# Sixteen ring slots: a 4 KB transfer scratch for GpSimd, and the norms' weight rows in the projection's output

## The chip, the cores and the metric

One core of one Trainium2 chip runs the kernel. The metric is device time in microseconds (us); the time before is the median of three runs. The engines named below are TensorE (PE, with its weight loads as PEld), VectorE (DVE), ScalarE (ACT), GpSimd (POOL) and SyncE (SP). SyncE issues nearly all transfers, GpSimd some fifty small ones.

## The reference

Everything is float32, with 256 tokens of width 1024. The first block is a hybrid layer with a mixture of experts, the second has two layers with a dense feed-forward each. Cut to what matters:

```python
# first block
mod = silu(c) @ w_ada + b_ada                      # six vectors of 1024
proj = (rms_norm(x, norm1_g) * (1 + scale1) + shift1) @ w_in
y = concat(conv(proj), stick_breaking(proj), forgetting(proj))
x = x + gate1 * ((head_rms(y) * out_norm_g) @ w_out)
h2 = rms_norm(x, norm2_g) * (1 + scale2) + shift2
for e in range(32):                                # top 4 of 32 for each token
    u = h2 @ w_mlp1[e] + b_mlp1[e]                 # 1024 x 2048
    acc += gate[e] * (swiglu(u) @ w_mlp2[e] + b_mlp2[e])   # 1024 x 1024
x = x + gate2 * acc
# second block
x = x + concat(fnet(p), conformer_conv(p)) @ w_out_ab     # p = rmsnorm(x) @ w_in_ab
x = x + swiglu_ffn(rmsnorm(x), w_gate, w_up, w_down)      # 1024 x 2816
x = x + pool_mixer(rmsnorm(x), pool_map) * pool_scale
x = x + swiglu_ffn(rmsnorm(x), w_gate, w_up, w_down)
return rmsnorm(x, final_g)
```

## The kernel before

All weights pass through one ring in SBUF. It has NRING slots of UNIT = 2048 float32 a partition, which is 1 MiB each. `ring_order` writes down, ahead of time, the order of all units and for each unit its slot, the semaphore value at which it has landed, and the units that held its slot before. A unit that is `wide` (all expert weights but the last expert's w2) takes two neighbouring slots and is one transfer of 2 MiB. SyncE goes through the same order: `fill` (line 3111 issues) waits until the slot's former units are emptied, and starts the transfer. It issues in order, so a fill that waits holds up all behind it. PE, DVE and ACT wait for a unit by its slot's semaphore.

The program runs through these parts:

- The front uses slots 0 to 7 for w_ada, w_in, then scale2, w_out. Slots 8 to 13 hold scratch of the front until its projection is done: `hTH`, `hTL` and the pieces `wp` of w_in, split in two rounded parts. `sp.wait_ge(*done(("in", "used", 31)))` stands ahead of gate2, which goes to slots 8 to 11.
- The experts: e = 0 to 31, in the order w1 of e (rows 2, 4, 6), the first w1 of e + 1, then the two w2 of e. Six wide units belong to one expert. TensorE (line 936 for w1, 954 for w2) multiplies up to 64 tokens of an expert, and up to 32 more in a second pass where it has them.
- The second block: w_in_ab (`abc`, `abr`), dft, fnet_map, w_out_ab, and gate, up and down of each feed-forward. It rotates through seven slots, since slots 7 to 13 hold the split hidden activations `FTH`, `FTL` and `HTH`.

Beside the ring lies one arena, a tensor of AW float32 a partition from which `al` hands out pieces. `o_rows` is the piece for seven norm weight vectors, one a partition. GpSimd loads them first (`small("rows", ...)`, line 2991), and TensorE turns them into columns at lines 585 and 588, before the modulation's last part and the projection. `o_P` is the piece `PJ`, the projection's output of 6144 float32 a partition. The rest of the arena is in use from front to end in changing roles.

GpSimd's own transfers are written by software into a descriptor scratch at the start of SBUF, 16 KB a partition by default. Its loads are the rows, biases and small vectors at the start, then the cumulated gates, the router's weights, and from 153 us the expert biases in_b_mlp (b1 and b2). ScalarE waits for b1 at line 2631, between its splits of the output projection's pieces.

```python
units[name] = (s, 16 * uses[s], [b for b in dict.fromkeys(before) if b is not None])
...
for prior in before:
    for step in emptied(prior):
        sp.wait_ge(*done(step))
sp.dma_start(view(ring[:, s * UNIT:(s + 1 + wide(name)) * UNIT]), src).then_inc(s_slot[s], 16)
```

Of the kernel before, what the change touches and what calls it, by code (L numbers as in the profile page):

```python
# [11 lines left out]
ACT = mybir.ActivationFunctionType  # L12
AX = mybir.AxisListType.X

NRING = 14
UNIT = 2048
NEXP = 32
CAP = 64
# [95 lines left out]
def w2_order(e):  # L114

    return (0, 2, 1, 3) if e == NEXP - 1 else (0, 2)


def wide(name):

    return name[0] == "w1" or name[0] == "w2" and name[1] < NEXP - 1


def front_order():

    order = []
    for n in range(16):
        order.append(("in", n // 2, n % 2))
        if 2 <= n < 10:
            order.append(("ada", 1, n - 2))  # L130
    return order


def ring_order():

    order = [("ada", 0, k) for k in range(8)] + front_order()
    first = len(order)
    order += [("scale2", k) for k in range(4)] + [("out", kk) for kk in range(4)] + [("gate2", k) for k in range(4)]
    experts = len(order)
    order += [("w1", 0, 0)]  # L140
    for e in range(NEXP):
        order += [("w1", e, k) for k in (2, 4, 6)]
        if e + 1 < NEXP:
            order += [("w1", e + 1, 0)]
        order += [("w2", e, k) for k in w2_order(e)]
    post = len(order)
    order += [("abc", c) for c in AB] + [("abr", kk) for kk in range(2)] + [("dft",), ("fm",)]
    order += [("outab", kk) for kk in range(4)]
    for l in range(2):
        if l:  # L150
            order += [("pool",), ("pmap",)]
        order += [(w, l, j) for j in range(NFF // 2) for w in ("gate", "up")]
        order += [("down", l, kk) for kk in range(NFF // 2)]
    units, uses, prior, at = {}, [0] * NRING, [None] * NRING, 0
    slots = list(range(8))
    for n, name in enumerate(order):
        if n == first:
            assert at % 2 == 0
            slots, at = [(at + i) % 8 for i in range(8)] + list(range(8, NRING)), 0
        if n == experts:  # L160
            slots, at = [12, 13, 0, 1, 2, 3, 8, 9, 10, 11, 4, 5, 6, 7], 0
        if n == post:
            slots, at = [4, 5, 6, 0, 1, 2, 3], 0
        s = slots[at % len(slots)]
        at += 1
        uses[s] += 3 if name[0] == "in" and name[1] >= 6 else 1
        before = [prior[s]]
        prior[s] = name
        if wide(name):
            t = slots[at % len(slots)]  # L170
            at += 1
            assert s % 2 == 0 and t == s + 1
            before.append(prior[t])
            prior[t] = name
        units[name] = (s, 16 * uses[s], [b for b in dict.fromkeys(before) if b is not None])
    return units


def build(nc, I, out, counts, counting):
    with ExitStack() as ctx:  # L180
        def sem(name):
            return ctx.enter_context(nc.semaphore(name))

        AW = 24536
        at_ring = -(-nc.sbuf_base // 32) * 32
        ring = ctx.enter_context(nc.sbuf_tensor("ring", [128, NRING * UNIT], F32))
        A = ctx.enter_context(nc.sbuf_tensor("arena", [128, AW], F32))
        at_arena = at_ring + NRING * UNIT * 4

        def rounded(name, at, n):  # L190
            return nc.alloc_sbuf_tensor_at(name, [128, n], F32R, offset=at)[:, :]
# [8 lines left out]
        sig["pool_front"] = Signal("pool_front", sem("s_pool_front"), counts)  # L200
        s_slot = [sem(f"s_slot{i}") for i in range(NRING)]
        s_load = {n: sem(f"s_load_{n}") for n in LOADS}

        def done(name):
# [4 lines left out]
            return sig[key].sem, n  # L209

        units = ring_order()

        def held(name):
# [18 lines left out]
        def al(n):  # L232
            o = top[0]
            top[0] += n
            assert top[0] <= AW, top[0]
            return o

        def v1(o, n, p0=0, p1=128):
            return A[p0:p1, o:o + n]
# [26 lines left out]
        def strided(rows, k):  # L266

            return rows[:, 256 * (k // 2) + k % 2:256 * (k // 2) + 256:2]
        o_rows = al(1024)
        NROW = len(ROWS)  # L270
        o_gc = al(8 * NROW)
        gcol = v1(o_gc, 8 * NROW).rearrange("p (k r) -> p k r", k=8)
# [11 lines left out]
        c8 = v1(o_c8, 128, 0, 8)  # L284

        o_P = al(6144)
        PJ = v1(o_P, 6144).rearrange("p (t n) -> p t n", t=2)
        o_hT = al(2304)
        hT = v1(o_hT, 2048).rearrange("p (k t) -> p k t", k=8)
# [45 lines left out]
        def in_view(b, t):  # L335
            if b < 6:
                return PJ[:, t, IN_COLS[b]:IN_COLS[b] + 384]
            return PJ[:, t, 0:768].rearrange("p (s c) -> p s c", s=3)[:, :, 128 * (b - 6):128 * (b - 6) + 128]

# [3 lines left out]

        vw = [[PJ[:, :, c:c + 128] for c in (CU + 128 * g, o, o + 128)] for g, o in enumerate((FK, SK))]
        hr = [v1(o_s1 + 16 + kind * 24, 24) for kind in range(2)]
# [93 lines left out]
        o_r = -(-(top[0]) // 8) * 8  # L439
        assert o_r + 2048 + 4096 <= AW and o_r <= o_cwr  # L440
        HTL = rounded("htl", at_arena + 4 * o_r, 2048).rearrange("p (k t) -> p k t", k=8)
# [4 lines left out]
        for q in range(4):  # L446
            at = at_arena + 4 * (o_r + 2048 * q if q < 2 else o_f + 2048 * (q - 2))
            ffn_bufs.append((rounded(f"wh{q}", at, 1024), rounded(f"wl{q}", at + 4096, 1024)))
        at = at_s
# [104 lines left out]
        def _(pe):  # L554
# [85 lines left out]
            def head_turn(kind, c0):  # L640
                pe.wait_ge(*done(("headed", kind)))
                pe.wait_ge(*done(("sb add", 0) if kind else "fB"))
                for m in range(3):
                    for c in (2 * m, 2 * m + 1):
                        for i in range(2):
                            o = (c % 2) * 256 + i * 128
                            t = pe.transpose(PS[:, 3 + m, o:o + 128], PJ[:, i, c0 + c * 128:c0 + (c + 1) * 128], ident)
                    t.then_inc(*P.tick(("heads turned", kind, m)))
# [29 lines left out]
            def weigh(g, bank, c_v, blocks, name):  # L678
                nh = len(HEADS[g])
                for hh, h in enumerate(HEADS[g]):  # L680
                    w00, w01, w11 = blocks(nh, hh)
                    vv = [PJ[:, i, c_v + h * 64:c_v + (h + 1) * 64] for i in range(2)]
                    oo = [PS[:, bank, (i * nh + hh) * 64:(i * nh + hh + 1) * 64] for i in range(2)]
# [856 lines left out]
        def _(dve):  # L1540
# [74 lines left out]
            def head_sum(kind, s):  # L1615
                dve.wait_ge(*done(("head squares", kind, s)))
                dve.tensor_reduce(hr[kind].rearrange("p (t h) -> p t h", t=2)[:, :, 6 * s:6 * s + 6],
                                  PJ[:, :, 384 * s:384 * s + 384].rearrange("p t (h d) -> p t h d", d=64), AX,
                                  ALU.add).then_inc(*V.tick(("head sums", kind, s)))
# [1603 lines left out]
def program(nc, arrays, counts, counting):  # L3223
    aps = {n: nc.dram_tensor(f"in_{n}", a.shape, mybir.dt.from_np(a.dtype), kind="ExternalInput").ap()
           for n, a in arrays.items()}
    out = nc.dram_tensor("out_0", (1, 256, 1024), F32, kind="ExternalOutput").ap()
    build(nc, aps, out, counts, counting)
# [14 lines left out]
```

## Time and profile before

| what | value |
|---|---|
| time, median of 3 runs (lowest, highest) | 1646.22 us (1643.47, 1648.41) |
| the profiled execution's own time | 1649.03 us |
| its span | 1647.3 us |
| TensorE busy | 1532.7 us, 93% |
| VectorE, ScalarE, GpSimd busy | 667.4, 454.0, 99.8 us |
| read from HBM | 530.87 MB |

The span is cut into stretches: the front and the output projection to about 190 us, routing to 204, the experts to about 1146, and the second block. A view by stretches gives for each engine the time that it was busy, and the rate of the DMA engines. Idle time stands at the engine that waited, with what released it.

### The profile page before, as it was taken

How to read it: one execution, taken by the hardware profiler on the slowest of the kernel's cores; microseconds unless marked ns; L12 is line 12 of the kernel's file. 1: busy time of each engine (PE TensorE's matmuls, PEld its weight loads, DVE VectorE, ACT ScalarE, POOL GpSimd, SP SyncE). 2: the span in 40 equal slices, each digit the busy share in tenths (PEclk: the TensorE clock that was granted, in tenths of full speed). 3: DMA queues.
4: the chain of work that ended last, by engine and by line, in shares of the span. 5: the costliest groups of instructions: out<-in, count | busy, mean ns of one | idle time of the engine just before them, and what ended most of it. 6: DMA issues, size and time to landing. Idle time of an engine off the chain costs nothing. (4 is left out here: it accounts for less than half of the span.)

```text
span 1647.3 us, 21485 instructions
## 1 busy us (share of the span) xinstructions
PE 1532.7 (93%) x8573; PEld 869.0 (53%) x8573; DVE 667.4 (41%) x960; ACT 454.0 (28%) x754; POOL 99.8 (6%) x114
## 2 busy tenths in 40 slices
PE   6999899999999988999998889886999999999998
PEld 3888633333333323333333323222858998789986
DVE  3576522232222222322221222223866565465654
ACT  3574411101111110111110101002865444354443
POOL 4032000000000000000000000000530000400000
PEclk8999899999999999999999999999999999999999
DMA  9977689999999999999999999999436555466540
GB/s 365 333 220 282 246 351 427 427 422 409 426 426 426 425 427 426 427 421 426 425 428 426 426 426 427 426 426 346 140 103 218 181 191 191 128 198 192 187 154 26
DMA packets 109695, 534.24 MB, mean 324 GB/s; under 512 B 6769, under 2 KB 69896, under 8 KB 83040
## 3 DMA queue, kind: packets, MB, share of 16 engines
q1 hardware_dynamic: 107600, 529.97, 81.1%
q8 instruction: 120, 1.97, 0.5%
q0 software_dynamic: 1936, 1.98, 0.4%
q14 instruction: 39, 0.32, 0.1%
HBM read 530.87 MB, written 1.05 MB: 323 GB/s over the span
## 5 line engine op out<-in xcount | busy, mean ns | idle before, releaser
L936 PE MATMUL ps<-ring,arena 128*64 128x512 f32 x2040 | 490.5, 606 | 21.8 <-DMA ring<-in_w_mlp 19.8
L936 PEld LDWEIGHTS ps<-ring,arena 128*64 128x64 f32 x2040 | 130.1, 137 | 261.7 <-issue 211.7
L954 PE MATMUL ps<-ring,arena 128*64 128x512 f32 x1024 | 230.9, 597 | 19.0 <-DMA ring<-in_w_mlp 11.6
L1546 DVE TENSOR_TENSOR wl<-ring,wh 128x1024 fp32r<-128x1024 f32 x132 | 162.0, 1232 | 135.2 <-ACT wh L2424 135.2
L541 PE MATMUL ps<-hth,wh 128*128 128x256 f32 x704 | 200.2, 284 | 1.9 <-DVE htl L2215 1.9
L542 PE MATMUL ps<-htl,wh 128*128 128x256 f32 x704 | 197.9, 281 | 0.0
L543 PE MATMUL ps<-hth,wl 128*128 128x256 f32 x704 | 197.3, 280 | 0.0
L2015 DVE TENSOR_TENSOR arena<-ps,arena 128x1024 f32<-128x1024 f32 x68 | 83.3, 1224 | 257.3 <-PE ps L961 250.6
L2424 ACT ACTIVATE wh<-ring 128x1024 fp32r<-128x1024 f32 x132 | 139.3, 1060 | 148.0 <-PE ps L543 148.0
L954 PEld LDWEIGHTS ps<-ring,arena 128*64 128x64 f32 x1024 | 74.1, 137 | 168.7 <-issue 142.3
L2040 DVE TENSOR_TENSOR arena<-ps,arena 128x512 f32<-128x512 f32 x34 | 23.5, 691 | 337.7 <-PE ps L954 334.5
L542 PEld LDWEIGHTS ps<-htl,wh 128*128 128x128 f32 x704 | 134.9, 192 | 0.0
L541 PEld LDWEIGHTS ps<-hth,wh 128*128 128x128 f32 x704 | 132.7, 189 | 2.6 <-DVE htl L2215 1.5
L543 PEld LDWEIGHTS ps<-hth,wl 128*128 128x128 f32 x704 | 133.8, 190 | 0.0
L2688 ACT ACTIVATE arena<-arena 128x512 f32<-128x512 f32 (+1 forms) x33 | 20.4, 617 | 306.4 <-DVE arena L2028 306.4
L2709 ACT ACTIVATE obh<-arena 128x512 fp32r<-128x512 f32 x30 | 18.9, 630 | 293.6 <-DVE arena L2040 286.6
L541 PE MATMUL ps<-wh,fth 128*128 128x512 f32 x176 | 69.7, 396 | 0.0
L542 PE MATMUL ps<-wl,fth 128*128 128x512 f32 x176 | 69.5, 395 | 0.0
L543 PE MATMUL ps<-wh,ftl 128*128 128x512 f32 x176 | 69.4, 394 | 0.0
L2669 ACT ACTIVATE arena<-ps,arena 128x256 f32<-128x256 f32 x60 | 30.6, 559 | 125.7 <-PE ps L907 118.4
L3078 POOL MEMSET arena<- 128x1144 f32 x1 | 1.1, 1063 | 998.9 <-DVE htl L2215 998.9
L541 PE MATMUL ps<-wp,ht 128*128 128x384 f32 (+1 forms) x128 | 45.9, 358 | 1.5 <-DVE wp L1546 1.4
(442 smaller groups left out, 1838.0 us busy)
## 6 DMA issues: line engine op xcount, KB each, us to landing
ring<-in_w_mlp SPq DMA_DIRECT2D x190, 2048.0 KB, 24.3
ring<-in_w_ada SPq DMA_DIRECT2D x24, 1024.0 KB, 11.0
ring<-in_ffn_w_gate SPq DMA_DIRECT2D x22, 1024.0 KB, 5.4
ring<-in_ffn_w_up SPq DMA_DIRECT2D x22, 1024.0 KB, 5.4
ring<-in_ffn_w_down SPq DMA_DIRECT2D x22, 1024.0 KB, 4.9
ring<-in_w_in SPq DMA_DIRECT2D x10, 768.0 KB, 12.2
ring<-in_w_in_ab SPq DMA_DIRECT2D x6, 1024.0 KB, 11.6
ring<-in_w_out SPq DMA_DIRECT2D x4, 1024.0 KB, 5.1
```

The costliest lines, as they stand in the source:

```text
L541: pe.matmul(o, lh, rh, start=first, stop=False)
L542: pe.matmul(o, lh, rl, start=False, stop=False)
L543: return pe.matmul(o, ll, rh, start=False, stop=last)
L936: t = pe.matmul(PS[64 * g:64 * g + 64, HB[hb][ns], :], x[:, k8, :], u[:, f:f + 512], start=False, stop=k8 == 7)
L954: t = pe.matmul(PS[64 * g:64 * g + 64, 3, :], a4[:, kc, 64 * kg:64 * kg + 64], u[:, c, g * 512:(g + 1) * 512], start=k8 == 0, stop=k8 == 7)
L1546: dve.tensor_tensor(l, src, h.bitcast(F32), ALU.subtract).then_inc(*V.tick((st, "lo", n)))
L2015: dve.tensor_tensor(x, PS[:, b:b + 2, :], x, ALU.add).then_inc(*tick(name))
L2040: dve.tensor_tensor(OBF, PS[:, bank, :], G2R, ALU.mult).then_inc(*tick(n_f))
L2424: act.activation(h, src, ACT.Copy).then_inc(*S.tick((st, "hi", n)))
L2669: act.activation(XGT[b % 2][:, k, :], PS[:, bank, (k % 2) * 256:(k % 2) * 256 + 256], ACT.Identity, scale=a2[:, k:k + 1], bias=sh2[:, k:k ...
L2688: act.activation(SIG[:, 0:n], GLU[:, 0:n], ACT.Sigmoid, scale=1.702).then_inc(*Q.tick(name))
L2709: act.activation(OBH[0], OBF, ACT.Copy).then_inc(*SM.same())
```

## The change

NRING goes from 14 to 16, and the ring takes 16 KB a partition more. The place comes from two sides. GpSimd's descriptor scratch is given as 4096 bytes a partition in place of the default 16384 (12 KB less), and the arena shrinks by 1024 float32 a partition (4 KB less), since `o_rows` is now the start of `o_P`. The lists of slots for the experts and for the second block get the new slots 14 and 15. The list at `first` grows by itself, but its twelve units use the same twelve slots as before.

```diff
@@ -12,7 +12,8 @@
 ACT = mybir.ActivationFunctionType
 AX = mybir.AxisListType.X
 
-NRING = 14
+NRING = 16
+SCRATCH = 4096
 UNIT = 2048
 NEXP = 32
 CAP = 64
@@ -158,9 +159,9 @@
             assert at % 2 == 0
             slots, at = [(at + i) % 8 for i in range(8)] + list(range(8, NRING)), 0
         if n == experts:
-            slots, at = [12, 13, 0, 1, 2, 3, 8, 9, 10, 11, 4, 5, 6, 7], 0
+            slots, at = [14, 15, 12, 13, 0, 1, 2, 3, 8, 9, 10, 11, 4, 5, 6, 7], 0
         if n == post:
-            slots, at = [4, 5, 6, 0, 1, 2, 3], 0
+            slots, at = [14, 15, 0, 1, 2, 3, 4, 5, 6], 0
         s = slots[at % len(slots)]
         at += 1
         uses[s] += 3 if name[0] == "in" and name[1] >= 6 else 1
@@ -181,7 +182,7 @@
         def sem(name):
             return ctx.enter_context(nc.semaphore(name))
 
-        AW = 24536
+        AW = 23512
         at_ring = -(-nc.sbuf_base // 32) * 32
         ring = ctx.enter_context(nc.sbuf_tensor("ring", [128, NRING * UNIT], F32))
         A = ctx.enter_context(nc.sbuf_tensor("arena", [128, AW], F32))
@@ -266,7 +267,6 @@
         def strided(rows, k):
 
             return rows[:, 256 * (k // 2) + k % 2:256 * (k // 2) + 256:2]
-        o_rows = al(1024)
         NROW = len(ROWS)
         o_gc = al(8 * NROW)
         gcol = v1(o_gc, 8 * NROW).rearrange("p (k r) -> p k r", k=8)
@@ -284,6 +284,7 @@
         c8 = v1(o_c8, 128, 0, 8)
 
         o_P = al(6144)
+        o_rows = o_P
         PJ = v1(o_P, 6144).rearrange("p (t n) -> p t n", t=2)
         o_hT = al(2304)
         hT = v1(o_hT, 2048).rearrange("p (k t) -> p k t", k=8)
@@ -3234,8 +3235,8 @@
     arrays = {n: np.ascontiguousarray(inputs[n]) for n in _INS}
     arrays.update(const=constants(), dft=dft_tables(), pool=pool_tables())
     counts = {}
-    program(_bacc.Bacc("TRN2", target_bir_lowering=False, num_devices=1), arrays, counts, True)
-    nc = _bacc.Bacc("TRN2", target_bir_lowering=False, num_devices=1)
+    program(_bacc.Bacc("TRN2", target_bir_lowering=False, num_devices=1, dynamic_dma_scratch_size=SCRATCH), arrays, counts, True)
+    nc = _bacc.Bacc("TRN2", target_bir_lowering=False, num_devices=1, dynamic_dma_scratch_size=SCRATCH)
     program(nc, arrays, counts, False)
     r = _run(nc, [{f"in_{n}": a for n, a in arrays.items()}], core_ids=[0])
     return r.results[0]["out_0"]
```

The order of the fills is the same in both kernels. What moves is what SyncE waits for ahead of each. On SyncE, from gate2 (in_w_ada, four fills) into the first experts, with the waits in brackets; s_pe_front and s_dve_oproj are steps of the front and the output projection, s_pe_moe and s_pe_w1b steps of the experts. Before:

```order
L3111 DMA ring<-in_w_ada 128x2x1024 [waits s_pe_front]
L3111 DMA ring<-in_w_ada 128x2x1024 x3
L3111 DMA ring<-in_w_mlp1 128x4096
L3111 DMA ring<-in_w_mlp1 128x4096 [waits s_pe_front] x4
L3111 DMA ring<-in_w_mlp2 128x4096 [waits s_dve_oproj] x2
L3111 DMA ring<-in_w_mlp1 128x4096 [waits s_pe_w1b,s_pe_moe] x4
L3111 DMA ring<-in_w_mlp2 128x4096 [waits s_pe_w1b,s_pe_moe]
```

The same place after the change:

```order
L3112 DMA ring<-in_w_ada 128x2x1024 [waits s_pe_front]
L3112 DMA ring<-in_w_ada 128x2x1024 x3
L3112 DMA ring<-in_w_mlp1 128x4096 x2
L3112 DMA ring<-in_w_mlp1 128x4096 [waits s_pe_front] x3
L3112 DMA ring<-in_w_mlp2 128x4096 [waits s_pe_front]
L3112 DMA ring<-in_w_mlp2 128x4096 [waits s_dve_oproj]
L3112 DMA ring<-in_w_mlp1 128x4096 [waits s_dve_oproj]
L3112 DMA ring<-in_w_mlp1 128x4096 [waits s_pe_w1b,s_pe_moe] x3
```

Two expert fills now wait for nothing instead of one, and eight instead of seven stand ahead of the first that waits for a step of the experts.

On SyncE, where the experts end and the second block's fills begin. Before:

```order
L3111 DMA ring<-in_w_in_ab 128x8x256 [waits s_pe_w1b,s_pe_moe] x3
L3111 DMA ring<-in_w_in_ab 128x8x256 [waits s_pe_w2b,s_pe_moe]
L3111 DMA ring<-in_w_in_ab 128x4x512 [waits s_pe_w2b,s_pe_moe] x2
L3111 DMA ring<-in_dft 128x896 [waits s_pe_w2b,s_pe_moe]
L3111 DMA ring<-in_fnet_map 128x4x128 [waits s_dve_mix]
L3111 DMA ring<-in_w_out_ab 128x2x1024 [waits s_dve_mix] x4
```

After the change:

```order
L3112 DMA ring<-in_w_in_ab 128x8x256 [waits s_pe_w1b,s_pe_moe] x2
L3112 DMA ring<-in_w_in_ab 128x8x256 [waits s_pe_w2b,s_pe_moe] x2
L3112 DMA ring<-in_w_in_ab 128x4x512 [waits s_pe_w1b,s_pe_moe] x2
L3112 DMA ring<-in_dft 128x896 [waits s_pe_w2b,s_pe_moe]
L3112 DMA ring<-in_fnet_map 128x4x128 [waits s_pe_w2b,s_pe_moe]
L3112 DMA ring<-in_w_out_ab 128x2x1024 [waits s_pe_w2b,s_pe_moe]
L3112 DMA ring<-in_w_out_ab 128x2x1024 [waits s_dve_mix] x3
```

fnet_map and the first w_out_ab now wait for steps of the last expert (s_pe_moe) and no longer for steps of the second block's mixer (s_dve_mix). On the other engines the instructions and their order are the same; where they wait for a slot's semaphore, the slot's number differs.

## Rows read from the trace of the kernel before

**Rows 1.** The page: span, TensorE, and DMA share in 40 slices.
```profile
span 1647.3 us, 21485 instructions
...
PE 1532.7 (93%) x8573; PEld 869.0 (53%) x8573; DVE 667.4 (41%) x960; ACT 454.0 (28%) x754; POOL 99.8 (6%) x114
...
DMA  9977689999999999999999999999436555466540
```

**Rows 2.** Busy time by stretch; last three columns: TensorE's clock, DMA share, GB/s.
```profile
140.00:190.00 50.00, 45.55 (x283) 33.92 (x283) 30.46 (x53) 21.88 (x39) 7.36 (x11) 0.97 1.00 389
190.00:210.00 20.00, 17.03 (x132) 11.85 (x129) 11.49 (x42) 7.25 (x15) 0.00 (x0) 0.83 0.01 5
210.00:240.00 30.00, 29.48 (x137) 9.84 (x135) 9.85 (x16) 4.95 (x8) 0.00 (x0) 1.00 0.98 381
240.00:370.00 130.00, 127.02 (x677) 45.02 (x673) 36.93 (x53) 14.14 (x28) 0.00 (x0) 1.00 1.01 426
370.00:390.00 20.00, 19.59 (x108) 6.16 (x106) 5.14 (x9) 2.66 (x5) 0.00 (x0) 1.00 0.96 386
390.00:510.00 120.00, 117.78 (x577) 41.70 (x573) 35.55 (x47) 14.14 (x28) 0.00 (x0) 1.00 1.01 426
510.00:710.00 200.00, 185.54 (x970) 63.55 (x968) 49.63 (x72) 20.45 (x40) 0.00 (x0) 0.99 1.01 426
710.00:720.00 10.00, 9.60 (x52) 3.58 (x50) 4.13 (x5) 1.84 (x4) 0.00 (x0) 1.00 0.99 408
720.00:1110.00 390.00, 354.08 (x1684) 121.05 (x1682) 98.39 (x129) 38.12 (x74) 0.00 (x0) 0.99 1.01 426
```

**Rows 3.** TensorE's waits, 205 to 510 us (first row), 510 to 1130 (others).
```profile
PE ps L945 <- DVE arena L2035: 4.6, 9, 0.5
...
PE ps L936 <- DMA ring<-in_w_mlp: 19.8, 18, 2.1
PE ps L954 <- DMA ring<-in_w_mlp: 11.6, 12, 1.8
...
PEld ps L936 <- DMA ring<-in_w_mlp: 44.1, 44, 3.0
...
PEld ps L954 <- DMA ring<-in_w_mlp: 25.6, 18, 2.7
```

**Rows 4.** Timeline of TensorE's weight loads, 1110 to 1128 us.
```profile
1112.62 0.20 PEld L954 LDWEIGHTS ps<-ring,arena 128*64 128x64 f32 x4 [2.70 <-DMA ring<-in_w_mlp]
...
1127.38 0.20 PEld L936 LDWEIGHTS ps<-ring,arena 128*64 128x64 f32 x4 [1.34 <-DMA ring<-in_w_mlp]
```

**Rows 5.** TensorE's only wait for a DMA from 1128 us on.
```profile
PE ps L936 <- DMA ring<-in_w_mlp: 0.5, 1, 0.5
```

**Rows 6.** Timeline of SyncE's issues: the first, sixth, seventh and eighth expert fill.
```profile
141.17 0.47 SPq L3111 DMA_DIRECT2D ring<-in_w_mlp  x1
...
164.71 0.33 SPq L3111 DMA_DIRECT2D ring<-in_w_mlp  x1
...
181.96 0.33 SPq L3111 DMA_DIRECT2D ring<-in_w_mlp  x1
...
209.50 0.33 SPq L3111 DMA_DIRECT2D ring<-in_w_mlp  x1
```

**Rows 7.** Timeline: the rows' turning, and the first write of projection output.
```profile
27.33 0.66 PE L585 MATMUL ps<-arena 7*128 7x7 f32 x8
...
41.88 0.81 ACT L2506 ACTIVATE arena<-ps 128x768 f32<-128x768 f32 x1 [2.35 <-DVE arena L1664]
```

**Rows 8.** GpSimd's queue on the page; then the view of tile in_b_mlp.
```profile
q0 software_dynamic: 1936, 1.98, 0.4%
...
L2991 POOL DMA_DIRECT2D arena<-in_b_mlp x6: 489/501/541, 153.2 to 156.7; - x6
...
  ACT b1s L2631: 1.6, 1
...
DMA to landing us min/median/max: 8.1/13.2/15.4
```

**Rows 9.** GpSimd's issues of in_b_ada, and their landing time in the list of transfers.
```profile
4.77 2.97 POOL L2991 DMA_DIRECT2D arena<-in_b_ada  x6
...
arena<-in_b_ada POOLq DMA_DIRECT2D x4, 4.0 KB, 5.1
```

## The prediction

> **What bounds the kernel now.** I read the page first. TensorE is busy for 1532.7 us of a span of 1647.3, and the line of DMA digits has a shape: nines at the start, a dip to 6, then nines for more than half of the span, then fours to sixes [rows 1]. So the kernel has at least three regimes, and a deeper ring is worth something only in those in which the transfers are late. The table by stretches tells them apart [rows 2]. From 140 to 190 us, while the first block's output projection runs, the DMA share is 1.00. From 190 to 210 us it is 0.01: the reader is to see a stretch in which SyncE has nothing that it may issue. From 210 to 1110 us, through 32 experts, the rate is 426 GB/s except in three places: 381 in 210 to 240, 386 in 370 to 390, 408 in 710 to 720.
>
> A full DMA does not yet say that the experts wait for it, since a ring that is always refilled also looks so. The waits of TensorE decide that. Between 205 and 510 us its longest kind of wait is 4.6 us for VectorE and there is none for a DMA. Between 510 and 1130 us it waits 19.8 + 11.6 = 31.4 us for expert weights, and its weight loads wait 44.1 + 25.6 = 69.7 us in spans that overlap those [rows 3]. So the first third of the experts runs at TensorE's pace and eats up the lead that the ring had; from about 510 us the stream sets the end. At the very end the cadence shows it: weight loads are released by an expert transfer at 1112.62, 1117.54, 1122.45 and 1127.38 us, of which the first and the last are shown [rows 4]. That is (1127.38 - 1112.62)/3 = 4.92 us for each transfer of 2048 KB. The other way to the same price: 2048 KB is 2.097 MB, and 2.097 MB at 426 GB/s is 4.92 us. After the last of these, TensorE's whole wait for DMA is 0.5 us [rows 5], so the 520 us behind the experts are not bound by transfers at all.
>
> **The change part by part.** The 44 fills ahead of the experts keep their slots and waits, and the first expert fill still waits for nothing. The first difference is the second expert fill: ("w1", 0, 2) now goes to slots 12 and 13 without a wait. From there on every wide fill waits for the release of the eighth wide fill before it, where it waited for the seventh.
>
> What that gives is read from SyncE's issues [rows 6]. Before, it has issued seven wide fills by 181.96 us, and the eighth waits until 209.50, when TensorE has emptied the first. The condition of the seventh, the release of the last two w_out units at 181.96 us, becomes that of the eighth; the seventh takes the condition of 164.71. So by 182 us eight wide fills are in the queue. The transfers run full to 190 us now; the eighth takes 4.92 us more and lands near 195, in a stretch that has a share of 0.01. The next fill is released at 209.50 as before, since TensorE's work up to there needs none of this. The stream therefore enters the experts one wide unit ahead.
>
> Does it keep that lead? While TensorE sets the pace, release times are what they were, a full ring is full with eight units instead of seven, and the DMA idles just as it did: the deficits of 210 to 240 and of 370 to 390 us (30 x 45 and 20 x 40 GB/s us, 1.35 and 0.80 MB) are ring-full stalls at TensorE's pace and stay. The lead after each is still one unit. From 390 us the stream runs full in both kernels. TensorE reaches it later, because it has one more unit in hand; of its 31.4 us of waiting the first 4.92 go away, and the rest is more than enough to turn a lead of 4.92 us into an end that is 4.92 us earlier. One stall more is recovered: at 710 to 720 us the ring was full again, and (426 - 408) x 10 = 0.18 MB, 0.42 us, were lost. There TensorE comes from a stretch in which it had waited, so it will be a unit further on and release in time. **Sum: 4.92 + 0.42 = 5.3 us.** An extra lead behind the experts is worth nothing: the waits for DMA there are 0.5 us, and w_in_ab, fnet_map and w_out_ab, which come earlier by their new conditions, are not waited for.
>
> The norms' rows in PJ cost nothing. TensorE turns them at 27.33 us; the first instruction that writes projection output is at 41.88 us [rows 7]. Engines run in order, the turning stands ahead of the projection on TensorE, so no wait is added; and the seven row loads are GpSimd's first issues in both kernels. If that cover of 14.5 us were gone, the projection would wait for the turning.
>
> GpSimd's scratch holds the descriptors of the transfers that it issues. It issues few: 1936 packets on its queue in the whole execution [rows 8], about 121 for each of the 16 DMA engines. The issues that matter are the six of in_b_mlp from 153.2 us: each takes about 0.5 us to issue and 8.1 to 15.4 us to land, and ScalarE already waits 1.6 us for them. Behind that wait stand its splits of the output projection's last four pieces, and behind these routing and the first expert. I cost it at nothing, with bounds in the third rival. The Trainium skill speaks against this edit. Its page SBUF — State Buffer, section on SBUF size, sets 16 KiB of each partition aside for this scratch and calls about 208 KiB usable, and its page DMA: Bandwidth & Descriptors (glossary) gives a descriptor 16 bytes. By that, 4 KB would hold 256 of them in a ring, an estimate from these pages, against the 121 packets an engine: the ring would not come round once, and the sum stays. No row of this trace shows the ring's fill. The DMA page also has a fit of 2.0 us plus bytes / 436e3 for a transfer; by its slope a unit would be 4.81 us, an estimate, and the sum 5.2. The measured cadence decides for 4.92.
>
> **The time.** The sum is made on the profiled execution, which took 1649.03 us with a span of 1647.3. Its span would become 1642.0. The median of the runs is 1646.22, 2.8 us below that execution; the same 5.3 us taken from it give 1640.9. What a measurement of this kernel can tell from no change is about 0.3%, 4.9 us. The forecast lies just beyond that, which makes faster and same nearly even inside my own case.
>
> **The rivals.** First, nothing is gained: the lead is eaten, because TensorE and not the stream is the bound over the whole of the experts. For it: from 205 to 510 us there is no wait for DMA, and TensorE is busy 354.1 of 390 us even from 720 to 1110 [rows 2]. Against it: the 31.4 us of waits, and the 4.92 us cadence in the last four. It gives 1646.2. 0.15.
>
> Second, more is gained: also the stalls at 210 to 240 and 370 to 390 us are filled by the deeper ring, 1.35 + 0.80 = 2.15 MB, 5.0 us. For it: a deeper queue smooths uneven releases. Against it: a full ring stays full when every release comes at the same time. All of it gives 1646.2 - 10.3 = 1635.9, the later stall alone (1.9 us) 1639.0, and this second value is the likelier. 0.12.
>
> Third, slower: GpSimd's issue stalls in its smaller scratch until earlier transfers have landed. The place is in_b_mlp at 153.2 us. The price is from nothing (1936 packets in all are few) up to six landings one behind the other, 6 x 13.2 = 79 us less the 15.4 of today, 64 us. The nearest row is one landing's median, 13.2 us: TensorE gets to the first expert so much later, the idle stretch of the DMA grows from 15 to 28 us, and the stream ends 13.2 - 5.3 = 7.9 us later: 1654.1. From a delay of 5.3 us on, this rival decides. Against it: at 4.77 us GpSimd issues six loads of in_b_ada in 2.97 us, each of which takes some 5.1 us to land, so it doesn't wait for landings [rows 9]. 0.06.
>
> That the change does not do what it says, because a fill in the new ring waits for a release that is later than I think, comes out as the first rival.
>
> **How the numbers follow.** My case has 0.67: 1640.9, and with 2 to 3 us of scatter between medians its own range is 1638.5 to 1643.5. The range reaches down to the second rival's likelier value less scatter and up to the first rival: 1637.5 to 1646.5. Below and above stay about 0.06 and 0.10. Faster by over 0.3% takes a little more than half of my case and all of the second rival, 0.37 + 0.12, and some of scatter, 0.50; same is the rest of mine and most of the first, 0.43; slower 0.07.
>
> **What the new profile would show.** SyncE issues eight expert fills of 2048 KB by 182 us and the ninth at 209.5. The 5 us behind 190 show a full DMA, the stretch from 195 to 209 none. The stretch 210 to 240 and the one near 370 to 390 keep their deficits; the one at 710 is gone. TensorE's first wait for an expert DMA comes after 510 us. The sum of its waits falls by about 5 us from 31.4, and the last release that read 1127.38 reads 1122. From there to the end it takes the same 520 us. The six in_b_mlp loads still land within 8 to 15 us. I am wrong if the last release has not moved (first rival), if the 381 and 386 GB/s have become 426 (second), or if the fill that now goes at 209.50 us goes later (third).

## The result, and the profile after

| | before | after |
|---|---|---|
| median | 1648.43 us (20 runs) | 1642.73 us (20 runs) |
| ratio | | 0.9969, 95% interval 0.9961 to 0.9978 |
| profiled execution's span | 1647.3 us | 1637.1 us |
| last release by an expert transfer | 1127.38 us | 1122.49 us |

The kernel became faster by 0.31%, which is 5.1 us; the forecast was 5.3. The medians in the table lie 5.7 us apart, somewhat more than the ratio on record says, and both lie inside its interval. As a time the forecast was 1640.9 us with a range of 1637.5 to 1646.5, taken from the 1646.22 of three runs. The kernel before came out at 1648.43 in its twenty, so it is the difference that can be compared. The two profiled spans differ by 10.2 us, twice as much. What of that belongs to the change is read at places, not from the spans.

SyncE's issues after the change, on the timeline. They answer to [rows 6]: the last of the eight, and the first that waits for an expert.

```profile
182.45 0.33 SPq L3112 DMA_DIRECT2D ring<-in_w_mlp  x1
...
210.01 0.33 SPq L3112 DMA_DIRECT2D ring<-in_w_mlp  x1
```

The fill at 210.01 us goes 0.5 us later than before, and a later fill there was named as a sign of the third rival. It is no sign at this size: in the nine profiled kernels that leave ScalarE's wait for b1 where it was (before, after, experiments 1 to 7) this fill goes between 207.91 and 210.72 us, and the earliest of them has the small scratch (experiment 1).

The stretches, with the columns of [rows 2]:

```profile
190.00:210.00 20.00, 17.03 (x138) 12.08 (x137) 11.52 (x41) 7.74 (x16) 0.00 (x0) 0.83 0.28 120
210.00:240.00 30.00, 29.49 (x133) 9.83 (x135) 9.81 (x16) 4.96 (x8) 0.00 (x0) 1.00 0.96 372
370.00:390.00 20.00, 19.59 (x112) 6.16 (x106) 4.88 (x9) 2.66 (x5) 0.00 (x0) 1.00 0.96 391
710.00:720.00 10.00, 10.00 (x51) 3.68 (x47) 3.51 (x4) 1.22 (x3) 0.00 (x0) 1.00 1.01 429
```

In 190 to 210 us the core's DMA engines now move 120 GB/s x 20 us = 2.4 MB where they moved 0.1: that is the eighth unit. Cut finer, it is 426 GB/s from 190 to 195 us and 2 GB/s from 200 to 209, as forecast. The deficits at 210 to 240 and 370 to 390 us are still there, and the one at 710 is gone, each as forecast. TensorE's waits for DMA between 510 and 1130 us:

```profile
PE ps L937 <- DMA ring<-in_w_mlp: 19.9, 17, 2.2
...
PE ps L955 <- DMA ring<-in_w_mlp: 9.3, 8, 1.8
...
PEld ps L937 <- DMA ring<-in_w_mlp: 42.6, 42, 3.1
...
PEld ps L955 <- DMA ring<-in_w_mlp: 21.9, 19, 2.6
```

The weight loads wait 64.5 us where [rows 3] have 69.7, 5.2 less, and the matmuls 29.2 where they had 31.4. The forecast of about 5 us less was for the matmuls' 31.4, and there it came to 2.2. Between the two events compared below, TensorE's idle time fell by 3.1 us (61.7 to 58.6) and the time counted as busy by 2.3 (856.2 to 853.9), with the same matmuls in both. The end of a matmul is modelled in the profile, so how the 5.4 us split into waiting and work is not shown; that TensorE passes the stretch so much sooner is.

The last release, on the timeline of the weight loads, which answers to [rows 4]:

```profile
1122.49 0.20 PEld L937 LDWEIGHTS ps<-ring,arena 128*64 128x64 f32 x4 [1.31 <-DMA ring<-in_w_mlp]
```

From the first fill that waits for an expert to this release it takes 1122.49 - 210.01 = 912.5 us, and 1127.38 - 209.50 = 917.9 before. The difference is 5.4 us. The measure scatters little: the four profiled kernels with seven units (before, experiments 1, 3, 9) have 917.8 to 918.8 us, and the five with eight that prefetch the eighth (after, experiments 2, 6, 7, 8) 912.5 to 913.1. It leaves out what the front did in either execution, and the experiments below are compared by it.

### The profile page after: what moved, and what is told of

It is laid out like the page before. It is cut to its first block and busy times, and to the rows that moved or that the text cites. A ratio compares the mean times of both kernels' runs of the same rounds, so it can differ in the third digit from the quotient of the medians.

```text
span 1637.1 us, 21486 instructions
## 1 busy us (share of the span) xinstructions
PE 1527.4 (93%) x8573; PEld 868.8 (53%) x8573; DVE 667.5 (41%) x960; ACT 454.2 (28%) x754; POOL 99.7 (6%) x114
## 5 line engine op out<-in xcount | busy, mean ns | idle before, releaser
L542 PE MATMUL ps<-wh,fth 128*128 128x512 f32 x176 | 69.7, 396 | 0.0
```

Source lines behind the costliest of these rows:

```text
L542: pe.matmul(o, lh, rh, start=first, stop=False)
```

## The experiments

**1. The room alone.** Scratch and rows as changed, ring and lists as before.

```diff
-NRING = 16
+NRING = 14
-slots, at = [14, 15, 12, 13, 0, 1, 2, 3, 8, 9, 10, 11, 4, 5, 6, 7], 0
+slots, at = [12, 13, 0, 1, 2, 3, 8, 9, 10, 11, 4, 5, 6, 7], 0
-slots, at = [14, 15, 0, 1, 2, 3, 4, 5, 6], 0
+slots, at = [4, 5, 6, 0, 1, 2, 3], 0
```

> The small scratch and the rows in PJ alone, with the ring and its slot lists as before (14 slots). My theory, that all of the gain comes through the ring: ratio to before 1.000, within 0.0010. Rival, that a part of the gain comes from the room itself (fewer or shorter delays of GpSimd's transfers, other addresses): 0.999 or less. Rival, that the small scratch costs something which the ring's gain hides: 1.001 or more, and in_b_mlp lands later than 15.4 us.

Measured: ratio 0.9998 (0.9983 to 1.0013); in_b_mlp lands in 7.4 to 15.0 us; 918.8 us from the first fill that waits for an expert to the last release. The room costs nothing that can be seen.

**2. and 3. The ring's depth in one half of the program.** Experiment 2 keeps the experts' list and takes the second block's from before; experiment 3 the reverse.

```diff
 # 2
-slots, at = [14, 15, 0, 1, 2, 3, 4, 5, 6], 0
+slots, at = [4, 5, 6, 0, 1, 2, 3], 0
 # 3
-slots, at = [14, 15, 12, 13, 0, 1, 2, 3, 8, 9, 10, 11, 4, 5, 6, 7], 0
+slots, at = [12, 13, 0, 1, 2, 3, 8, 9, 10, 11, 4, 5, 6, 7], 0
```

> Sixteen slots for the experts, the second block with its seven slots as before. My theory: the whole gain, ratio 0.9969, last release by an expert transfer at about 1122.5 us. Rival, that the second block gains from its nine slots (the profiled span of the changed kernel was 5 us shorter behind the experts too): 0.9985.

> Fourteen slots for the experts, nine in place of seven for the second block. My theory: ratio 1.000, within 0.0010, last expert release at 1127 us. Rival, that the second block gains too: 0.9985, with the time from the last expert release to the end 3 to 5 us under 520.

Measured: the experts' list alone 0.9966 (0.9951 to 0.9981), 912.7 us. The second block's alone 0.9991 (0.9979 to 1.0002), 918.1 us. All of the gain that can be measured is in the experts. The interval of the second leaves room for a gain of up to 0.2% but does not show one, and the trace has no wait for it.

**4. The eighth fill held.** It keeps its slot, and waits besides for the release of the first unit.

```diff
         units[name] = (s, 16 * uses[s], [b for b in dict.fromkeys(before) if b is not None])
+    units[("w1", 1, 2)][2].append(("w1", 0, 0))
```

> All sixteen slots, but the eighth expert fill, which went at 182 us into the idle stretch, is held until TensorE has emptied the first, at 210. Theory A, my prediction's words (the stream enters the experts one unit ahead, and the gain is made in the idle stretch): the gain is gone, ratio 1.000. Theory B (what counts is how many units the ring holds when it is last full at TensorE's pace, near 380 us; up to there the stream has spare time of 1.35 + 0.80 = 2.15 MB, one unit, to catch up): ratio 0.997 to 0.998, the deficits at 210 to 240 and 370 to 390 us filled to 426 GB/s, last expert release at 1122.5 to 1123.

Measured: 0.9974 (0.9962 to 0.9986), last release at 1125.71 us, 915.0 us after the first fill that waits for an expert (210.72). Its stretches:

```profile
190.00:210.00 20.00, 17.10 (x130) 12.18 (x128) 11.72 (x43) 8.44 (x18) 0.00 (x0) 0.83 0.05 20
210.00:240.00 30.00, 29.41 (x152) 10.24 (x150) 9.70 (x15) 4.42 (x8) 0.00 (x0) 1.00 0.95 393
370.00:390.00 20.00, 19.60 (x114) 6.03 (x108) 4.83 (x9) 2.66 (x5) 0.00 (x0) 1.00 1.01 428
```

The idle stretch stays idle, and yet 2.9 of the 5.4 us are gained. Theory A is out in its words (the gain is gone), but the other 2.5 us do need the idle stretch. Theory B is half right: the ratio is as expected, the last release came at 1125.71 where it expected 1122.5 to 1123. The stall at 370 to 390 us is filled (428 GB/s). At 210 to 240 us (426 - 393) x 30 = 0.99 MB are still missing, and finer slices show where: 220 GB/s from 210 to 215 us and 428 from 215 to 240. So this is the stream's start after the idle stretch, and no stall of a full ring. Of the 2.15 MB that were missing before, 2.15 - 0.99 = 1.16 MB are won back, 2.7 us, near the 2.9 measured. The kernel before has the same start: 318 GB/s from 210 to 215 us, so (426 - 318) x 5 = 0.54 of its 1.35 MB belong to it and not to a full ring.

**5. Six units.** Two pairs of slots less in the experts' list.

```diff
-slots, at = [14, 15, 12, 13, 0, 1, 2, 3, 8, 9, 10, 11, 4, 5, 6, 7], 0
+slots, at = [14, 15, 0, 1, 2, 3, 8, 9, 10, 11, 4, 5], 0
```

> The changed kernel with two pairs of slots taken from the experts' list (12 and 13, 6 and 7): six wide units where before had seven and the change has eight. The same theory with the other sign, one unit less of lead at the last full ring: 4.9 us longer than before, and the stall near 715 us, which eight units took away, grows. Ratio to before 1.003 to 1.004. Rival, a threshold (eight is just enough to even out TensorE's bursts, and below it each expert stalls the stream): 1.006 or more, with the rate under 426 GB/s throughout the experts.

Measured: 1.0025 (1.0013 to 1.0037). First fill at 210.44, last release at 1133.35 us, 922.9 us. The ratio lies a little below the 1.003 to 1.004 that I expected, and its interval reaches into them. The stall near 715 us has grown as forecast:

```profile
700.00:710.00 10.00, 10.00 (x48) 3.42 (x50) 1.12 (x3) 1.31 (x3) 0.00 (x0) 1.00 0.99 408
710.00:720.00 10.00, 9.60 (x60) 2.50 (x56) 3.99 (x5) 1.26 (x2) 0.00 (x0) 1.00 0.98 395
```

So six, seven and eight units give 922.9, 917.9 and 912.5 us: one unit is 5.0 to 5.4 us, nearly a straight line, and there is no threshold at eight. The rate from 720 to 1110 us is 426 GB/s with all three, against the rival's expectation. The stalls do not add up as simply as the prediction's sum has it: in 700 to 720 us six units lose 0.49 MB where seven lose 0.20, 0.7 us more, but at 370 to 390 us they lose 0.36 MB where seven lose 0.80, 1.0 us less. The first matmul that waits for an expert DMA moves with the depth. On the timelines of six units, of before and of after:

```profile
496.23 3.65 PE L937 MATMUL ps<-ring,arena 128*64 128x512 f32 x16 [1.39 <-DMA ring<-in_w_mlp]
```
```profile
549.83 3.65 PE L936 MATMUL ps<-ring,arena 128*64 128x512 f32 x16 [0.41 <-DMA ring<-in_w_mlp]
```
```profile
599.61 0.65 PE L955 MATMUL ps<-ring,arena 128*64 128x512 f32 x2 [1.17 <-DMA ring<-in_w_mlp]
```

**6. and 7. A smaller scratch.** The changed kernel with `SCRATCH = 1024`, and with `SCRATCH = 576`.

> The changed kernel with 1024 bytes of scratch for GpSimd in place of 4096, nothing else. If the scratch never runs full, because GpSimd's transfers are few and their descriptors are taken up at once: ratio 0.997, in_b_mlp lands in 7.5 to 16 us and each issue takes 0.5 us as before. My third rival, at its own place: at some size the issues of in_b_mlp or of the first twenty-odd loads stall. Then an issue takes several us, in_b_mlp lands later, ScalarE waits longer than 2.0 us for it, and the ratio is 0.998 or more; at one landing of 13 us it would be 1.005.

> The changed kernel with 576 bytes of scratch. At 1024 bytes there was a first sign: a gap of 0.23 us between the second and third in_b_mlp issue, which no other run has. If that is the scratch running full, 576 bytes make it larger: gaps of 1 us or more between GpSimd's issues in the first 15 us and at in_b_mlp, b1 lands later, ScalarE waits longer than 2.0 us, TensorE gets to the first expert later by as much, and the ratio rises from 0.997 to 0.998 to 1.005. If the gap was chance: no gaps, ratio 0.997, and the third rival has no place in this kernel at any size that it can have.

Measured: 0.9963 (0.9951 to 0.9976) at 1024 bytes and 0.9972 (0.9960 to 0.9984) at 576, both as the changed kernel within their intervals. At 576 bytes GpSimd's timeline shows one gap among its first loads that no other run has:

```profile
10.44 0.96 POOL L2992 DMA_DIRECT2D arena<-in_fox_q_g  x2 [0.78 <-issue]
```

The gap is 0.78 us, under the 1 us that I expected, and nobody waits for these loads. At in_b_mlp there is no gap at 576 bytes, so the 0.23 us at 1024 does not come from the size of the scratch alone. in_b_mlp lands in 7.4 to 14.9 and 8.3 to 16.0 us. The first part of what I expected of 576 bytes came on a small scale and the chain from there to a later first expert didn't. The gap fits a scratch that ran full; that it was this is argued, not shown.

**8. ScalarE waits for b1 later.** In the profile after, ScalarE waits 2.0 us for b1 and copies it for 1.1 us, ahead of the splits that TensorE needs. The edit moves both behind two of them.

```diff
+            for n in range(4, 6):
+                hi("out", n)
             act.wait_ge(s_load["b1"], 64)
             act.wait_ge(*done(("y turned", 3)))
             act.activation(B1S, B1raw, ACT.Copy).then_inc(*S.tick("B1H"))
-            for n in range(4, 8):
+            for n in range(6, 8):
                 hi("out", n)
```

> The changed kernel with ScalarE's wait for b1 and its copy (3.1 us together in the profile after) moved behind the splits of w_out pieces 4 and 5, where it idles 4.8 us anyway. TensorE waits 3.2 us for piece 4 there and then runs six matmuls at the lower clock (0.63 for 0.39 us). My theory says that whatever makes TensorE reach the first expert earlier shortens the idle stretch of the DMA and moves the whole stream: the first fill that waits for an expert goes at 206 to 207 instead of 210 us, the last expert release at 1118.5 to 1119.5, ratio to before 0.9945 to 0.995. Rival, the stream alone sets the end of the experts and an earlier start of TensorE is worth nothing: 0.9969.

Measured: 0.9951 (0.9938 to 0.9965), 1639.71 us against 1647.46 for before on the same chip. That is faster than before; that it is also faster than the changed kernel (0.9969, 0.9961 to 0.9978) whole runs leave open, since the intervals overlap by a little and experiment 6, the changed kernel with a smaller scratch, has 1642.20 us on the same chip in eight runs against six. The trace shows it. TensorE after the change, on the timeline:

```profile
172.89 0.79 PE L542 MATMUL ps<-wo,yh 128*128 128x512 f32 x1 [3.19 <-DVE wo L1547]
173.48 0.63 PE L543 MATMUL ps<-wo,yh 128*128 128x512 f32 x1
```

and with the later wait, where the piece is there 0.5 us after the last matmul's start and the matmuls stay at the upper clock (2.4 GHz; the granted share is 1.00 from 170 to 174 us, and 0.57 from 172 to 176 in the changed kernel):

```profile
169.52 0.39 PE L544 MATMUL ps<-wo,yl 128*128 128x512 f32 x1
170.04 0.50 PE L542 MATMUL ps<-wo,yh 128*128 128x512 f32 x1
170.37 0.39 PE L543 MATMUL ps<-wo,yh 128*128 128x512 f32 x1
```

The piece is taken up 172.89 - 170.04 = 2.9 us earlier, and the seventh matmul from there starts at 171.53 us where the changed kernel has 175.61, 4.1 earlier: 1.2 us more is what the lower clock had cost. The first fill that waits for an expert goes at 205.27 us, 4.7 earlier, and the last release is at 1117.96, 4.5 earlier; between them lie 912.7 us. Both came earlier than the windows that I had given, and the ratio just outside its own, 0.9945 to 0.995. In the trace the rival, that an earlier start of TensorE is worth nothing in a stretch that the stream bounds, is out; in whole runs the next experiment puts it out.

**9. The same in the ring of fourteen slots.** The edit of 8 together with the slot lists and NRING of 1.

> The later wait for b1 in the ring of fourteen slots. If TensorE's earlier start (4.7 us, as with sixteen slots) and the eighth unit are two separate shifts of the same stream, they add: ratio 0.9970 to 0.9978, last expert release at 1122.5 to 1123.5, and from the first fill that waits for an expert to the last release 918 us as in every kernel with seven units. Rival, the earlier start is worth something only with the eighth unit in the ring: ratio 0.999 or more, last release at 1126 to 1127.

Measured: 0.9969 (0.9958 to 0.9981), first fill at 207.72, last release at 1125.49 us, 917.8 us between them. The last release misses the window, because the whole front was 2.6 us late in this execution (in_b_mlp goes at 155.8 us, 153.2 before); from in_b_mlp to the first fill it takes 51.9 us where before has 56.3, 4.4 less. Experiment 8 has 51.7, and the nine kernels without the later wait have 54.5 to 57.0, so the gain at this place is clear of their scatter. In whole runs the two gains are of one size, 0.9969 each. That they add is shown by the traces: the first fill comes earlier by the later wait, and the time from it to the last release is 917.8 us with seven units and 912.7 with eight, as without it. Whole runs do not settle it: 0.9969 x 0.9969 = 0.9938 lies at the edge of the interval of experiment 8.

## Why the prediction was right, by its steps

**The bound.** TensorE first, then the stream from some place between 510 and 600 us on (the first matmul that waits for the stream is at 549.83), was read from the waits alone, and all of the steps rest on it. Experiment 5 shows it from outside: a unit of ring is worth one transfer's time only if the stream sets the end.

**The price of a unit**, 4.92 us, plus 0.42 for the stall at 710 us, against 5.4 measured between first fill and last release. The stall is gone in the trace after. The 0.42 by itself is not shown, since it is smaller than the scatter of the measure and experiment 5 shows other stalls changing with the depth. The forecast took the 5.3 us out of the matmuls' waits, which fell by 2.2 only; that the price came right all the same does not rest on this step. The fit that the prediction took from the Trainium skill (DMA: Bandwidth & Descriptors) is given there for transfers that GpSimd issues, these are SyncE's, and the measured 4.92 us stays the price. In whole runs the ratio says 5.1 us, with an interval of 3.6 to 6.4.

**Where the lead comes from.** Here the words of the prediction were too narrow. It said that the stream enters the experts one unit ahead, and that the lead is kept because a full ring idles the same. Both are what happened, but experiment 4 shows that about half of the gain would have come without the first. With the eighth fill held, the stream has no stall left at 370 to 390 us: the deeper ring no longer fills there, and the stream catches up 2.9 us and no more. With the eighth unit fetched in the idle stretch, the ring is full again near 380 us, now with eight, and the whole 5.4 us are there. So depth and prefetch are both needed for the whole gain. The second rival (the stalls at 210 and 370 us filled by a deeper ring) did not happen in the changed kernel, for the reason given. Its price was set too high, though: the prediction read all of the 1.35 MB at 210 to 240 us as stalls of a full ring, and 0.54 MB of it is the start of the stream.

**Nothing behind the experts.** Experiments 2 and 3 bear it out within their intervals. The profile alone would have said otherwise: from the last release to the end it takes 514.6 us after, not 520. Over eleven profiled kernels this part takes 514.6 to 520.3 us. Its mean is 517.8 for the four kernels with the second block's old list (before, experiments 1, 2, 9) and 518.0 for the seven with the new one. The executions of before and after, 519.9 and 514.6, happen to lie near opposite ends.

**The rows in PJ and the scratch at nothing.** Experiment 1: 0.9998. The third rival, a stall of GpSimd's issues, had no place at 4096 bytes. Even at 576 bytes, a seventh of that, it has left the time where it was. The Trainium skill's 16 KiB (SBUF — State Buffer, section on SBUF size) is what the default sets aside; this kernel runs on a quarter of it at no cost that can be measured. The estimate of 256 descriptors a ring against 121 packets an engine agrees with that, but does not explain it: the same estimate gives 64 at 1024 bytes and 36 at 576, under the 121, and those kernels are as fast.

**The first rival**, nothing gained, is out by the ratio's interval and by experiments 2 and 5.

## What to carry to other kernels

In front of a stream that bounds the later part of a long stage, one more transfer of ring paid that transfer's time here (six, seven and eight were measured), once for the whole stage, and depth did not raise the rate. It pays in full only where the stream has idle time early on in which to fill it. So look at the places where the ring was full and the stream stood, since this is what a deeper ring can win back. Whatever lets the consumer reach its first release earlier (here a wait for a bias, moved by two splits on ScalarE) moves the stream with it, here 4.7 us at the first release and 4.5 at the last, and costs no memory. Compare two profiles between two events of the same stage, since whole spans of single executions differ by more than a gain of this size.

## What the runs showed of the hardware that was not expected

Between the last expert and the second block TensorE's clock either stays at its upper level or falls, whatever the kernel. The same eight matmuls, on the timelines of before, of after, and of experiment 8:

```profile
1134.17 3.26 PE L954 MATMUL ps<-ring,arena 128*64 128x512 f32 x8 [0.62 <-ACT arena L2734]
```
```profile
1129.28 1.94 PE L955 MATMUL ps<-ring,arena 128*64 128x512 f32 x8 [0.62 <-ACT arena L2735]
```
```profile
1124.76 2.75 PE L955 MATMUL ps<-ring,arena 128*64 128x512 f32 x8 [0.62 <-ACT arena L2737]
```

In all three TensorE had stood idle for 0.6 us just in front, so that does not tell them apart, and what does stays open. The granted clock over the 12 us from 1128 us is 0.86, 1.00 and 0.78 of the upper level, 2.4 GHz; experiment 8 is then further on in its work by 9.4 us than before. From the last release to the second block's first matmuls (L1242) it takes 16.2 us in six of the eleven kernels and 17.8 to 19.1 in the others. That alone moves a span by up to 2.9 us, and it explains that much of the 10.2 us between the two profiles; 5.4 us are the change's, the front was 0.5 us later after the change, and what is left, 2.4 us, lies in the second block and was not taken apart.
